# Scanning 64 candidate pairs in place of 256 in the product-key search of a decoder step

## What is computed

```
s1, i1 = lax.top_k(s[:, :, 0], PEER_TOPK)        # best 16 of 128, first side
s2, i2 = lax.top_k(s[:, :, 1], PEER_TOPK)        # best 16 of 128, second side
cand_s = (s1[..., :, None] + s2[..., None, :]).reshape(T, PEER_HEADS, n_cand)      # 256 sums
cand_i = (i1[..., :, None] * PEER_NKEYS + i2[..., None, :]).reshape(T, PEER_HEADS, n_cand)
top_s, top_pos = lax.top_k(cand_s, PEER_TOPK)
e_idx = jnp.take_along_axis(cand_i, top_pos, axis=-1)
gate = jax.nn.softmax(top_s, axis=-1)
```

## Time and profile before

| | |
|---|---|
| median of 3 runs | 3245.22 us (3241.13 to 3252.75) |
| the profiled execution | 3243.07 us |
| its span, first to last instruction | 3241.0 us |
| mean granted PE clock | 0.985 |
| PE busy | 3143.3 us (97% of the span) |
| DVE busy | 2379.3 us (73%) |
| ACT busy | 995.1 us (31%) |
| POOL busy | 796.9 us (25%) |
| key search stage | about 743 to 1149 us of the span |
| decode stage | about 1149 to 1250 us |

### The profile page before, as it was taken

One profiled execution on the slowest core, in us unless ns is written; L12 is line 12 of the kernel. 1 busy time (PEld: TensorE's weight loads), 2 busy tenths in 40 slices (PEclk: granted clock), 3 DMA queues, 4 the chain that ended last, 5 costly groups with the idle time before them and its releaser, 6 DMA issues. The chain is left out here.

```text
span 3241.0 us, 49377 instructions
## 1 busy us (share of the span) xinstructions
PE 3143.3 (97%) x17258; PEld 2775.6 (86%) x17258; DVE 2379.3 (73%) x5085; ACT 995.1 (31%) x1487; POOL 796.9 (25%) x588
## 2 busy tenths in 40 slices
PE   6999999799999999999999999999999999999999
PEld 4777777578999999999999999977888888888887
DVE  5676555445999768999577777648888888888886
ACT  4323333222222123444222222223333334333333
POOL 0000000001111100000376656534333333433330
PEclk9999999899999999999999999999999999999999
DMA  4111110222221223778999999989999999999993
GB/s 164 41 47 58 55 41 28 92 92 96 72 72 59 69 92 115 241 239 259 334 412 377 369 360 360 353 299 403 364 353 352 357 354 392 383 356 352 353 351 139
DMA packets 324580, 754.30 MB, mean 233 GB/s; under 512 B 22456, under 2 KB 154044, under 8 KB 323312
## 3 DMA queue, kind: packets, MB, share of 16 engines
q1 hardware_dynamic: 145024, 408.29, 34.6%
q0 software_dynamic: 79776, 290.00, 23.7%
q10 hardware_dynamic: 99664, 54.56, 5.7%
HBM read 637.82 MB, written 114.95 MB: 232 GB/s over the span
## 5 line engine op out<-in xcount | busy, mean ns | idle before, releaser
L1251 PE MATMUL u_p<-hn_hi,u_hi 128*128 128x384 f32 x2048 | 699.4, 342 | 7.4 <-PEq L1274 3.7
L1253 PE MATMUL u_p<-hn_hi,u_lo 128*128 128x384 f32 x2048 | 692.9, 338 | 0.0
L1252 PE MATMUL u_p<-hn_lo,u_hi 128*128 128x384 f32 x2048 | 692.6, 338 | 0.0
L1941 POOL DMA_INDIRECT y_ring<-in_peer_v,row_idx x248 | 367.5, 1482 | 624.8 <-DVE yt L2083 574.8
L1745 POOL DMA_INDIRECT s_ring<-in_peer_u,row_idx x264 | 334.8, 1268 | 620.2 <-DVE row_idx L1838 411.7
L1987 PE MATMUL y_p<-v_hi,w_hi 128*128 128x512 f32 x1536 | 474.5, 390 | 10.4 <-DVE w_lo L2074 10.4
L1989 PE MATMUL y_p<-v_lo,w_hi 128*128 128x512 f32 x1536 | 474.2, 390 | 0.0
L1992 PE MATMUL y_p<-v_hi,w_lo 128*128 128x512 f32 x1536 | 473.7, 390 | 0.0
L1251 PEld LDWEIGHTS u_p<-hn_hi,u_hi 128*128 128x128 f32 x2048 | 386.0, 188 | 9.4 <-issue 7.4
L1252 PEld LDWEIGHTS u_p<-hn_lo,u_hi 128*128 128x128 f32 x2048 | 386.2, 189 | 0.0
L1253 PEld LDWEIGHTS u_p<-hn_hi,u_lo 128*128 128x128 f32 x2048 | 386.1, 189 | 0.0
(11 more groups left out here) (350 smaller groups left out, 4694.4 us busy)
## 6 DMA issues: line engine op xcount, KB each, us to landing
u_raw<-in_peer_ut SPq DMA_DIRECT2D x128, 512.0 KB, 7.7
late<-in_peer_v SPq DMA_DIRECT2D x64, 1024.0 KB, 7.4
down_raw<-in_peer_v SPq DMA_DIRECT2D x64, 1024.0 KB, 7.2
act_scratch<-act_tile SPq DMA_DIRECT2D x128, 384.0 KB, 5.7
gate_scratch<-gbuf ACTq DMA_DIRECT2D x6, 4096.0 KB, 16.4
gate_scratch<-late ACTq DMA_DIRECT2D x6, 4096.0 KB, 20.8
late<-act_scratch SPq DMA_DIRECT2D x64, 384.0 KB, 8.6
late<-gate_scratch SPq DMA_DIRECT2D x64, 384.0 KB, 10.3
```

The source lines that it names most:

```text
L1251: mm(b, uh[:, s, k, :], hn_hi[:, k, t], start=(k == 0), stop=False)
L1252: mm(b, uh[:, s, k, :], hn_lo[:, k, t], start=False, stop=False)
L1253: last = mm(b, ul[:, s, k, :], hn_hi[:, k, t], start=False, stop=(k == ND - 1))
L1941: nc.gpsimd.indirect_dma_start(out=ring[:, n % RING, :], out_offset=None, in_=A["peer_v"], in_offset=bass.IndirectOffsetOnAxis(ap=idx[:, N ...
```

## The change

The 256 sums become 64, laid out as four rectangles that cover every pair that can be among the best sixteen: pair rows 0; 1 to 3; 4 to 7; 8 to 15 with 16, 8, 4 and 1 columns. `cand` is written by four instructions a group, and the five scans a tile run over 64 elements. The place is now a slot 0 to 63, and the decode works a and b back from it: a is the largest of (slot / 8) - 1, (slot / 4) - 6, slot - 48 and 0; `edge` is the slot at which row a begins; b is the slot less `edge`. That is one more conversion (`slot`) beside the first ones and nine linked instructions of 1,152 elements behind the conversion of L1580, ahead of `u_low(dve, E0 + 1, 1)`. The mask with 15 of L1576 becomes a shift by 2. `slot` and `edge` use memory that is free at that point (`gt`, and the place of `left`). No other engine's list is changed.

```diff
+RECTS = [(0, 1, TOPK, 0), (1, 3, 8, 16), (4, 4, 4, 40), (8, 8, 1, 56)]
+NCAND = 64
-            cand = sb(st, "cand", [P, 4, TOPK * TOPK])
-            crest = sb(st, "crest", [P, 4, TOPK * TOPK])
+            cand = sb(st, "cand", [P, 4, NCAND])
+            crest = sb(st, "crest", [P, 4, NCAND])
-                    ch.mark(v.tensor_tensor(
-                        cand[:r, 0:G, :].rearrange("p q (a b) -> p q a b", b=TOPK),
-                        tv[:r, 0:G, 0, :].unsqueeze(3).broadcast_to([r, G, TOPK, TOPK]),
-                        tv[:r, 0:G, 1, :].unsqueeze(2).broadcast_to([r, G, TOPK, TOPK]), ALU.add))
+                    for a0, na, nb, at in RECTS:
+                        ch.mark(v.tensor_tensor(
+                            cand[:r, 0:G, at:at + na * nb].rearrange("p q (a b) -> p q a b", b=nb),
+                            tv[:r, 0:G, 0, a0:a0 + na].unsqueeze(3).broadcast_to([r, G, na, nb]),
+                            tv[:r, 0:G, 1, 0:nb].unsqueeze(2).broadcast_to([r, G, na, nb]), ALU.add))
+            slot, edge = gt, late[:, 6 * NT * K8:7 * NT * K8].rearrange("p (t k) -> p t k", k=K8)
-                ch.mark(v.tensor_scalar(ab_u[:, :, 0, :], pos, 4, None, ALU.logical_shift_right))
-                ch.mark(v.tensor_scalar(ab_u[:, :, 1, :], pos, TOPK - 1, None, ALU.bitwise_and))
+                ch.mark(v.tensor_scalar(ab_u[:, :, 0, :], pos, 3, None, ALU.logical_shift_right))
+                ch.mark(v.tensor_scalar(ab_u[:, :, 1, :], pos, 2, None, ALU.logical_shift_right))
+                ch.mark(v.tensor_copy(slot[:, :, :], pos))
                 ch.mark(v.tensor_copy(i1[:, :, :, :, :].rearrange("p t i h k -> p (t i h k)"),
                                       ti[:, :, :, :, :].rearrange("p t i h k -> p (t i h k)")))
                 ch.wait(ch.n)
                 ch.link(v.tensor_copy(ab[:, :, :, :].rearrange("p t i k -> p (t i k)"),
                                       ab_u[:, :, :, :].rearrange("p t i k -> p (t i k)")))
+                a, b = ab[:, :, 0, :], ab[:, :, 1, :]
+                ch.link(v.tensor_scalar(a, a, -1.0, 0.0, ALU.add, ALU.max))
+                ch.link(v.scalar_tensor_tensor(a, b, -6.0, a, ALU.add, ALU.max))
+                ch.link(v.scalar_tensor_tensor(a, slot[:, :, :], -48.0, a, ALU.add, ALU.max))
+                ch.link(v.tensor_scalar(edge[:, :, :], a, 8.0, 8.0, ALU.mult, ALU.add))
+                ch.link(v.scalar_tensor_tensor(edge[:, :, :], a, 16.0, edge[:, :, :], ALU.mult, ALU.min))
+                ch.link(v.tensor_scalar(b, a, 4.0, 24.0, ALU.mult, ALU.add))
+                ch.link(v.tensor_tensor(edge[:, :, :], edge[:, :, :], b, ALU.min))
+                ch.link(v.scalar_tensor_tensor(edge[:, :, :], a, 48.0, edge[:, :, :], ALU.add, ALU.min))
+                ch.link(v.tensor_tensor(b, slot[:, :, :], edge[:, :, :], ALU.subtract))
                 dve.wait_ge(ident_done, 1)
                 u_low(dve, E0 + 1, 1)
```

## The result

| | before | after |
|---|---|---|
| median of 12 runs | 3249.98 us (3241.13 to 3260.76) | 3263.01 us (3252.84 to 3266.06) |
| the profiled execution | 3243.07 us | 3266.02 us |
| its span | 3241.0 us | 3264.2 us |

The change makes the kernel slower: the ratio is 1.0035, interval 1.0021 to 1.0049, which on 3250 us is 11.4 us (6.8 to 15.9). The same kernel in a later series of runs (experiment 1) gave 1.0025 (1.0012 to 1.0038).

The account below looks back on a forecast made before the run. PE was taken to set the pace, with DVE having a little slack in the search. The terms -1.85 + 10.7 + 2.0 = +10.85 us led to a forecast of 3255.0 us, range 3249 to 3262 us.

Parts of the forecast that it names:

- a stall of 10.7 us: Start of the decode: PE stands still for block 23's remainder, 12.5 less 1.78 us; ends 10.0 and 12.4.
- The scans: Search on DVE: five scans a tile each 0.2 us shorter, some 72 us less busy with `cand`, nothing on the path.
- A sign that failed: Search: in the profile after, DVE's waits for PE's scores were to be far above 13.6 us.
- The sample picks: End of the search: `picks_done` comes earlier, SP's 8.9 us wait and PE's 1.59 us stall go, gaining 1.85 us.
- The chain: Start of the decode on DVE: ten added instructions ahead of block 23's remainder cost 12.5 us, ends 11.8 and 14.2.
- The cover: Start of the decode: block 23's remainder was ready 1.78 us before PE came to it.
- No second wait: Decode after the stall: block 24's remainder is ready 0.46 us early at full clock, so PE sets the pace.
- The clock: Decode after the stall: PE restarts at a reduced clock and loses 2.0 us, ends 1.6 and 2.6.
- the hidden pace: Rival, search: DVE's groups really hold up PE's starts, up to 70 us faster, 3184 us; chance 0.03.
- the covered chain: Rival, decode: the added instructions cost under 1.78 us or PE has other work, 3241.2 us; chance 0.04.
- the second wait: Part of a rival with long instruction forms: PE late again if DVE's work to block 24 grows over 0.46 us; chance 0.12.
- a cost that does not fall with the width: Rival, search: a fixed cost per instruction keeps the scans from shortening, no search gain, 3255.8 us; chance 0.03.

Follow-up runs that it names:

- experiment 1: The kernel after run again with no edit, against the kernel before: 3254.47 us, ratio 1.0025.
- experiment 2: The kernel after with the decode of before (shift by 4, mask with 15, no `slot`, no nine linked instructions): 3245.99 us, ratio 0.9993.
- experiment 3: The kernel before with the ten added decode instructions on scratch memory, its search unchanged: 3261.84 us, ratio 1.0037.
- experiment 4: The kernel after with block 23's remainder taken ahead of the nine linked instructions instead of behind them: 3254.61 us, ratio 1.0023.
- experiment 8: The kernel after with the turning back of places moved into the search, the sample tile's behind the decode's first tile: 3243.55 us, ratio 0.9989.

## Why the prediction was right

I had forecast a stall of 10.7 us, 2.0 us of clock and a gain of 1.85 us. They measured 10.41, 1.41 and 1.9 in the first profile, a sum of +9.9 us against my +10.85. The mechanism came as written; the sizes of two terms and one of the signs did not.

- **The scans.** 0.2 us less for each was right (419 to 219 ns). The four rectangles take 0.224 + 0.249 + 0.224 + 0.182 = 0.88 us in place of 1.235, within my bounds. DVE's window lost 74.8 us, and I had 72 for the search. That none of it is on the path, apart from the sample picks, was right, and experiment 2 shows it alone.
- **A sign that failed.** I had said that DVE's waits for scores would be far above 13.6 us. They were 22.6; most of the freed time went into the wait for ACT, 85.1 us in place of 29.9, which my account of what DVE waits for left out. It changes nothing in the sum, since either way DVE waits and PE does not.
- **The sample picks.** The wait for `picks_done` and the 1.59 us stall are gone. Search: 406.7 us before and 406.7 in experiment 3; 404.8 to 405.4 in the eight profiles that have the search of the kernel after unaltered, so 1.3 to 1.9 us against my 1.85.
- **The chain.** It grew by 12.13 us (to the end of the remainder of block 23, 20.53 us after DVE's first instruction of the decode; 8.40 before). I had 12.5. The term mis-sized was scalar_tensor_tensor, 1.36 us and not 1.42, four times: 0.24 of the 0.37. My row was one with a scalar for each partition; with two constants it took what a tensor_tensor takes, 1.36. The choice between short and long form came out as I had put it, and as the mode rule of the Trainium skill ("VectorE: DVE Perf Modes", the section on mode 2x_2P) states: 0.83 and 0.82 us for the two on equal strided shapes, 1.35 for the one from strided to flat.
- **The cover** of 1.78 us was there: PE's wait begins when block 22 ends, and 12.13 - 1.78 = 10.35 is the 10.41 measured.
- **No second wait**: none in the profile, as forecast; the remainder of block 24 was early.
- **The clock** cost 1.4 to 2.1 us after a stall of this length (four profiles), against 2.0 with ends 1.6 and 2.6. The lower end was set too high.
- **The total.** The ratio 1.0035 stands for 11.4 us; the sum was 10.85. That they agree within 0.6 us is in part luck: the stages gave 9.9, and the later series' 1.0025 stands for 8.1 us. The median itself, 3263.01 us, lies 1 us above the range. The mechanism is not the reason: the kernel before measured 3249.98 us in the same runs and not 3245.22. On three runs I had given the baseline too little spread; the mixer alone varies by 15 us between executions.

The rivals: the hidden pace is excluded by experiment 2, the covered chain by experiment 3, the second wait by the profiles after (one wait of PE for a vector remainder in each), a cost that does not fall with the width by the rows.

## What to carry to other kernels

Work taken from an engine that is not the bound is worth only what someone waits for. Before simplifying such an engine's work at the price of a conversion elsewhere, look at what stands behind the conversion in its list at that moment: 75 us saved under cover were outweighed by 12 us in a place with 1.8 us of cover. Putting block 23's remainder ahead in the same list only moved the stall (experiment 4); moving the work to where the slack is removed it (experiment 8). And a whole-kernel difference of 10 us is better read from the lengths of the stages, which repeated within 0.7 us in the search, than from two spans of which an untouched stage can shift one by 12.

## What was not expected of the hardware

- A subtraction on POOL made a DVE tensor_scalar last 2.90 us and not 0.82, and a DVE scalar_tensor_tensor 2.63 us and not 0.42; a scalar_tensor_tensor under way made POOL's 3.46 us and not 2.4. Moving work to an idle POOL was no free relief.
- The same stage with the same instructions can take 614 or 629 us. In the stretches shown the granted clock was 0.91 to 1.00, and the shorter executions were the ones with the higher clock.
- The restart of PE lost 1.4 to 2.1 us of clock after a 10 us standstill and 2.4 to 2.6 us after 22 us, but also 1.3 to 2.9 us after one of about 4 us. Why is left open.
